# Experts' weights in 22 places for 17, column quarters in the gate and up products, and picks for one group of experts at a time

## The chip, the cores and the metric

The kernel runs on one core of a Trainium2 chip. Five engines work side by side and wait for each other through semaphores: TensorE (PE, matmuls into the eight banks of PSUM), VectorE (DVE), ScalarE (ACT), GpSimd (POOL) and SyncE (SP, which here issues all transfers, in order). The metric is the device time of one execution in microseconds. A smaller one is better.

## The reference

Two transformer blocks follow each other on 256 tokens of width 1024. The first has four feed-forward layers, a convolution and a latent attention; the second has a gated recurrence and an attention beside it, and then a mixture of 16 experts. The change lies in the experts. All weights are float32.

```python
def expert_choice_moe(h, w_router, w_gate, w_up, w_down):
    cap = EC_CAPACITY_FACTOR * length // N_EXPERTS        # 2 * 256 // 16 = 32 rows an expert
    aff = jax.nn.softmax((h @ w_router).astype(jnp.float32), axis=-1)
    gate, idx = lax.top_k(jnp.swapaxes(aff, 1, 2), cap)
    xe = h[bidx, idx]
    hid = jax.nn.silu(jnp.einsum("becd,edf->becf", xe, w_gate)) * jnp.einsum("becd,edf->becf", xe, w_up)
    ye = jnp.einsum("becf,efd->becd", hid, w_down) * gate[..., None].astype(h.dtype)
    return jnp.zeros_like(h).at[bidx, idx].add(ye)

        # behind the token mixing of the second block:
        x = x + g2 * expert_choice_moe(modulate(rms_norm(x, norm2_g[l]), sh2, sc2),
                                       w_router[l], w_exp_gate[l], w_exp_up[l], w_exp_down[l])
    return rms_norm(x, final_norm_g)
```

Each expert has three matrices of 1024 x 1024, so the experts' weights are 201 MB of the 427 MB that the kernel moves.

## The kernel before

Every engine has a program written out by hand, and SP's program is the order of all weights. A weight is loaded in pieces of 1 MB, [128 partitions x 2048], called slots or tiles. Up to the experts all pieces go through `ring`, six slots that are used in turn: PE raises the semaphore `slot_free` by one with the last matmul of a piece (`done`), and SP waits for that count before it loads piece n + 6 (`wait_free`). One SBUF region, `arena`, is laid out anew for every phase.

An expert has 12 tiles: four of the gate matrix, four of up, four of down (m = 0, 1, 2 in `product(m, j, src)`). Tile j holds rows 256 j to 256 j + 255, two to a partition (k = 0, 1). A product has 32 rows, so a matmul uses 32 of the array's columns, and four go to the four column groups of the array, into PSUM partitions 32 g on. Before the change they are the two k and the two halves of 512 output columns, so the results of the two k stand in different partitions: ScalarE copies one of them out of PSUM (`half_g_ready`, `half_u_ready`, `half_y_ready`) and VectorE adds the other.

Where expert tiles go before the change: 6 ring slots and 6 tiles `ahead` are used in turn (`EXP_SLOTS` is 12), and 5 `extra` tiles are used once, by the first five tiles of expert 1. That makes 17. SP loads two tiles into the ring while the branches run, waits for `merged_ready` (the two branches of the second block are added), loads the six ahead and then the rest as `w_out` frees ring slots, then the row of the final gain, and then tile after tile as places come free (`reused_load`).

The steps of the phase ahead, with the semaphores that the change uses: `hg_normed` (the recurrence's output is normed; its inputs are spent), `att_ready` (the attention's queries and keys are turned), the attention's blocks, two units of `branch` a and two of `branch` b (L1126), the four units of `w_out` (L1160), routing and seeding of the result in PSUM banks 0 to 3 (`h_seeded`), the choice of 32 tokens per expert (VectorE), then expert 0.

The chosen rows are gathered by matmuls with 0/1 `picks` (`gather`, L1213), for four experts at once (`GROUP`), into `x_exp`; in the kernel before this happens behind experts 1, 2 and 3 for the three later groups, and `x_cur` holds a copy of the rows of the expert in work. `spread` (L1221) turns the picks of one expert, scaled by its gates, and the last four matmuls of an expert (L1285) add its rows into banks 0 to 3. Behind the last expert the rows are squared and summed (ScalarE), scaled (VectorE) and stored. From expert 4 on all engines run a loop.

## Time and profile before

| | us |
|---|---|
| median of 3 runs | 1898.05 |
| lowest and highest | 1891.79, 1898.17 |
| the profiled execution's own time | 1893.91 |
| its span in the profile | 1892.1 |
| PE, PEld, DVE, ACT busy | 1733.2, 1376.9, 824.0, 673.2 |
| chain that ended last: PE, DMA, DVE, ACT | 77%, 14%, 4%, 3% |

The busy times are unions of the time in which the engine had an instruction in work. The chain is followed back from the last instruction, at each step to what released it. The profile cuts the span into 40 slices of 47.3 us and gives busy shares and transfer rates for each; the experts are the last ten. Rates of windows that are asked for are in GB/s, and a DMA share of about 1.0 says that all 16 DMA engines of the core worked all the time.

### The profile page before, as it was taken

The numbers are of one execution on the slowest core, as the hardware profiler recorded it, in microseconds if no ns is written. First come the engines' busy times: TensorE is split into PE (matmuls) and PEld (weight loads), VectorE is DVE, ScalarE is ACT, GpSimd is POOL, SyncE is SP. The second block draws the span as 40 slices with busy tenths as digits, with TensorE's granted clock in tenths as the row PEclk, the third lists the DMA queues.
The fourth block names the chain that finished last, engine by engine and source line by source line (L and its number), as shares of the span: only waits on it lengthen the run. The fifth ranks groups of instructions, "written<-read, shape, count | busy, mean of one in ns | idle before, by whom it ended". The sixth has DMA issues, their size and how long they took to land.

```text
span 1892.1 us, 28745 instructions
## 1 busy us (share of the span) xinstructions
PE 1733.2 (92%) x11907; PEld 1376.9 (73%) x11913; DVE 824.0 (44%) x1164; ACT 673.2 (36%) x976; POOL 10.7 (1%) x8
## 2 busy tenths in 40 slices
PE   8999999999999999999999999998998777767666
PEld 7999987999999999778999856886785332121212
DVE  6555697855566555134655504722422111111111
ACT  5444556644454443133444323315503221111111
POOL 0000010000000000000000000000000000000000
PEclk9999999999999999999999999999998887877777
DMA  9655455465546554544555452321179999999997
GB/s 300 226 175 186 157 187 185 134 200 177 183 151 200 180 187 149 159 130 142 193 191 185 156 157 88 112 90 67 45 285 376 397 422 422 422 422 422 422 422 325
DMA packets 200309, 427.12 MB, mean 226 GB/s; under 512 B 9187, under 2 KB 147861, under 8 KB 175668
## 3 DMA queue, kind: packets, MB, share of 16 engines
q1 hardware_dynamic: 200244, 426.19, 62.2%
q8 instruction: 48, 0.79, 0.2%
q14 instruction: 17, 0.14, 0.0%
HBM read 425.12 MB, written 1.05 MB: 225 GB/s over the span
## 4 chain that ended last, share of the span: by engine, by line
PE 77%; DMA 14%; DVE 4%; ACT 3%; SPq 1%; issue 1%; DVEq 0%; ACTq 0%
PE banks L621 14%; PE banks L622 14%; PE banks L623 14%; DMA ring<-in_w_exp_up 14%; PE banks L1247 4%; PE banks L995 4%; PE banks L971 3%; PE banks L792 2%; PE banks L744 1%; PE banks L1126 1%; PE banks L976 1%; PE banks L1160 1%; SPq L563 1%; PE banks L839 1%; PE banks L653 1%; PE banks L1213 1%
## 5 line engine op out<-in xcount | busy, mean ns | idle before, releaser
L621 PE MATMUL banks<-x_split,w_split 128*128 128x256 f32 x1600 | 457.1, 286 | 10.2 <-DVE x_split L1870 4.2
L622 PE MATMUL banks<-x_split,w_split 128*128 128x256 f32 x1600 | 453.4, 283 | 0.0
L623 PE MATMUL banks<-x_split,w_split 128*128 128x256 f32 x1600 | 453.3, 283 | 0.0
L1853 DVE TENSOR_TENSOR w_split<-ring,w_split 128x1024 fp32r<-128x1024 f32 x288 | 346.5, 1224 | 237.7 <-ACT w_split L1351 237.2
L1351 ACT ACTIVATE w_split<-ring 128x1024 fp32r<-128x1024 f32 x287 | 295.1, 1051 | 190.1 <-PE banks L623 188.2
L621 PEld LDWEIGHTS banks<-x_split,w_split 128*128 128x128 f32 x1600 | 307.8, 192 | 13.5 <-issue 6.0
L622 PEld LDWEIGHTS banks<-x_split,w_split 128*128 128x128 f32 x1600 | 307.7, 192 | 0.3
L623 PEld LDWEIGHTS banks<-x_split,w_split 128*128 128x128 f32 x1600 | 307.8, 192 | 0.0
L621 PE MATMUL banks<-hid_split,w_split 128*128 128x256 f32 x704 | 199.6, 284 | 0.0
L622 PE MATMUL banks<-hid_split,w_split 128*128 128x256 f32 x704 | 199.2, 283 | 0.0
L623 PE MATMUL banks<-hid_split,w_split 128*128 128x256 f32 x704 | 199.2, 283 | 0.0
L1247 PE MATMUL banks<-ring,arena 128*32 128x512 f32 x720 | 132.6, 834 | 42.2 <-DMA ring<-in_w_exp_up 35.1
L621 PEld LDWEIGHTS banks<-hid_split,w_split 128*128 128x128 f32 x704 | 135.1, 192 | 0.7 <-DVE hid_split L1922 0.7
L623 PEld LDWEIGHTS banks<-hid_split,w_split 128*128 128x128 f32 x704 | 135.1, 192 | 0.0
L622 PEld LDWEIGHTS banks<-hid_split,w_split 128*128 128x128 f32 x704 | 135.1, 192 | 0.0
L1247 PE MATMUL banks<-arena 128*32 128x512 f32 x728 | 107.6, 706 | 11.6 <-DMA arena<-in_w_exp_up 9.5
L1247 PEld LDWEIGHTS banks<-ring,arena 128*32 128x32 f32 x720 | 23.0, 132 | 108.8 <-DMA ring<-in_w_exp_up 71.9
L995 PE MATMUL banks<-xn,ring 128*128 128x256 f32 x448 | 99.4, 380 | 1.3 <-ACT arena L1612 0.7
L995 PEld LDWEIGHTS banks<-xn,ring 128*128 128x128 f32 x448 | 84.3, 190 | 13.9 <-issue 1.2
L1247 PEld LDWEIGHTS banks<-arena 128*32 128x32 f32 x728 | 26.4, 127 | 87.6 <-issue 56.1
L1400 ACT ACTIVATE hid_split<-gated 128x512 fp32r<-128x512 f32 x44 | 27.8, 632 | 150.4 <-DVE gated L1920 150.4
L2441 DVE TENSOR_TENSOR arena<-banks,arena 64x512 f32<-64x512 f32 x16 | 10.9, 683 | 152.8 <-ACT arena L1753 152.8
(371 smaller groups left out, 1893.5 us busy)
## 6 DMA issues: line engine op xcount, KB each, us to landing
ring<-in_ffn_w SPq DMA_DIRECT2D x131, 1024.0 KB, 5.3
arena<-in_w_exp_gate SPq DMA_DIRECT2D x58, 1024.0 KB, 24.4
ring<-in_w_exp_up SPq DMA_DIRECT2D x47, 1024.0 KB, 25.9
ring<-in_w_exp_down SPq DMA_DIRECT2D x45, 1024.0 KB, 24.5
ring<-in_w_mod SPq DMA_DIRECT2D x24, 1024.0 KB, 5.2
ring<-in_w_in SPq DMA_DIRECT2D x21, 1024.0 KB, 5.3
arena<-in_w_exp_down SPq DMA_DIRECT2D x19, 1024.0 KB, 26.0
arena<-in_w_exp_up SPq DMA_DIRECT2D x16, 1024.0 KB, 26.3
```

Source lines behind the costliest of these rows:

```text
L563: sp.dma_start(view, src).then_inc(full, 16)
L621: mm(out_, hi, moving(0), start=start, stop=False, **kw)
L622: mm(out_, hi, moving(1), start=False, stop=False, **kw)
L623: return mm(out_, lo, moving(0), start=False, stop=stop, **kw)
L653: last = mm(ps[:, bank, 0:n], ones[:, 0:P], squares[:, first + i, 0:n], start=(i == 0), stop=(i == k_tiles - 1))
L792: mm(ps[:, b, c:c + T], diag[:, q % DIAGS, :], conv_in[:, j, w:w + T], start=(w == 0), stop=(w == CONV_W - 1)).then_inc(sem("diag_used"), 1)
L971: last = mm(ps[:, b + o, :], slot(n)[:, k * 256 + o * P:k * 256 + o * P + P], xn[:, k, :], start=(k == 0), stop=(k == KD - 1))
L995: last = mm(ps[:, b, o * T:o * T + T], slot(n)[:, k * 256 + o * P:k * 256 + o * P + P], x_in[:, k, :], start=(k == 0), stop=(k == KD - 1))
L1247: last = mm(ps[g:g + 32, 4 + m, :], src(2 * j + k), w[:, k * D + 512 * half:k * D + 512 * half + 512], start=(j == 0), stop=(j == 3))
L1351: fn(half_part(n, o, 0), half_slot(n, o, columns), ACT.Copy).then_inc(sem("half_hi"), 1)
L1400: fn(hid_split[:, c % 2, 0, :, :], hidden[:, c % 2, :, :], ACT.Copy).then_inc(sem("hid_hi"), 1)
L1853: ins = dve.tensor_tensor(half_part(n, o, 1), half_slot(n, o, columns), half_part(n, o, 0).bitcast(F32), ALU.subtract)
```

## The change

The change has four parts.

- **Places.** The 12 + 5 places become 22 `tiles`, all used in turn by `tile_load(i)`: tile i of the 192 goes to place i % 22. Room for them comes from tensors whose contents are spent: `squares`, `gated`, `xn`, `h`, ten pieces of `arena` and the ring. The small tensors of the experts go to `roots` (std and rstd), `consts` and `att_stat`. The final gain's row goes last.
- **When they are asked for.** SP asks for tiles 0 and 1 behind `hg_normed`, 2 to 6 behind `att_ready`, 7 to 9 and 10 behind branch a, 11 and 12 behind branch b's units, 13 and 14 behind `merged_ready`, 15 to 18 as `w_out` frees ring slots, 19 and 20 behind its end and 21 behind `h_seeded`. The loads of `w_out` 2 and 3 now stand behind seven and ten of them.
- **Column quarters.** For gate and up a matmul has 256 output columns for 512, and the four column groups hold the four quarters; both k add up in PSUM. A tile has eight matmuls for four, the copy and the add of the halves are gone, and the activation works on [128 x 256]. Down has halves still, with its two k in different groups; their sum is left to the last four matmuls, which now contract 64 rows for 32, so the spread has 8 matmuls for 4 and the gate rows are 128 wide for 64.
- **Rows of one group.** `picks` holds four experts, computed anew by VectorE at experts 1, 5 and 9; the gather of a group comes behind experts 3, 7 and 11. `pick_cur` is computed by VectorE from the slots; `x_cur` is gone. All loops over experts are written out.

```diff
-        picks = r4.take(2 * TT, EXPERTS, CAP)
-        pick_cur, x_cur, spread_cur = r4.take(TT, CAP), r4.take(KD, CAP), r4.take(T)
-        choice = r4.take(6, T)
+        x_exp = laid(arena[:, 0:KD * GROUP * CAP], KD, GROUP * CAP)
+        choice = laid(roots[:, :], 4, T)
+        gate_e, hid_e = choice[:, 0, :], choice[:, 1, :]
+        y_e = choice[:, 2:4, :].rearrange("p a t -> p (a t)")
         work_a, work_b, chosen, slot_t = (choice[:, i, :] for i in range(4))
...
-        AHEAD = SLOTS
-        ahead = r4.take(AHEAD, SLOT)
-        once = r4.take(2, SLOT)
+        spent = consts[:, CONST["headsum"][0]:CONST["axial_sin"][1]]
+        picks = laid(spent[:, 0:TT * GROUP * CAP], TT, GROUP * CAP)
+        spread_cur = spent[:, 256:512]
+        hid_t = laid(spent[:, 512:768], KD, CAP)
+        pick_cur = laid(spent[:, 768:832], TT, CAP)
-        extra = [gated[:, :, :].rearrange("p a c -> p (a c)"), once[:, 0, :], once[:, 1, :],
-                 squares_flat[:, 0:SLOT], squares_flat[:, SLOT:2 * SLOT]]
-        EXTRA = len(extra)
-        EXP_SLOTS = SLOTS + AHEAD
-        REUSED = 12 * (EXPERTS - 1) - EXTRA
+        arena_tile = {a: arena[:, a:a + SLOT] for a in (1024, 3072, 5120, 7168, 9216, 11264, 13312, 15360, 17920, 19968)}
+        tiles = [squares_flat[:, 0:SLOT], gated[:, :, :].rearrange("p a c -> p (a c)")] + \
+                [arena_tile[a] for a in (7168, 9216, 11264, 17920, 19968, 1024, 3072, 5120)] + [squares_flat[:, SLOT:2 * SLOT]] + \
+                [ring[:, (N_EXPERTS + q) % SLOTS, :] for q in range(2)] + [arena_tile[a] for a in (13312, 15360)] + \
+                [ring[:, (N_EXPERTS + q) % SLOTS, :] for q in range(2, SLOTS)] + [xn_flat[:, 0:SLOT], xn_flat[:, SLOT:2 * SLOT]] + \
+                [h[:, :, :].rearrange("p k t -> p (k t)")]
+        TILES = len(tiles)
+        RING_TILES = (11, 12, 15, 16, 17, 18)
+        GAIN_TILE = 12 * (EXPERTS - 1)
+        gain_row = tiles[GAIN_TILE % TILES][:, 0:D]
...
-            def reused_load(u, more=None):
-                q, s = u % EXP_SLOTS, (u + EXTRA) % 12
-                used = u + 1 if u < EXP_SLOTS else u - EXP_SLOTS + 12 + EXTRA + 1
-                sp.wait_ge(slot_free, FIRST["experts"] + used + (0 if more is None else 12 * more))
-                expert_load(expert_view(q), s, 1 + (u + EXTRA) // 12, expert_full(q)[0], more)
-            for s in range(2):
-                wait_free(sp, FIRST["experts"] + s)
-                first_load(s)
+            def tile_load(i):
+                sp.dma_start(tiles[i % TILES], exp_tiles[i % 12][i // 12]).then_inc(tile_full(i % TILES)[0], 16)
+            def w_out_load(j):
+                cols(FIRST["w_out"] + j, w_out_2[0], 256 * j, 256, KD)
+            w_out_load(0)
+            w_out_load(1)
+            sp.wait_ge(sem("hg_normed"), 1)
+            for i in range(2):
+                tile_load(i)
+            sp.wait_ge(sem("att_ready"), 1)
+            for i in range(2, 7):
+                tile_load(i)
+            w_out_load(2)
+            sp.wait_ge(slot_free, FIRST["branch"] + 1)
+            for i in range(7, 10):
+                tile_load(i)
+            w_out_load(3)
+            sp.wait_ge(slot_free, FIRST["branch"] + 2)
+            tile_load(10)
+            for i in range(11, 13):
+                wait_free(sp, N_EXPERTS + RING_TILES.index(i))
+                tile_load(i)
             sp.wait_ge(sem("merged_ready"), 2)
-            for s in range(SLOTS, SLOTS + AHEAD):
-                first_load(s)
-            for s in range(2, SLOTS):
-                wait_free(sp, FIRST["experts"] + s)
-                first_load(s)
-                for b in ((0, 1, 2), (3, 4), (), ())[s - 2]:
-                    expert_load(extra[b], b, 1, sem("extra_in"))
+            for i in range(13, 15):
+                tile_load(i)
+            for i in range(15, 19):
+                wait_free(sp, N_EXPERTS + RING_TILES.index(i))
+                tile_load(i)
+            sp.wait_ge(slot_free, FIRST["w_out"] + 4)
+            for i in range(19, 21):
+                tile_load(i)
             sp.wait_ge(sem("h_seeded"), TT)
+            tile_load(21)
+            for i in range(TILES, 12 * EXPERTS):
+                sp.wait_ge(slot_free, N_EXPERTS + i - TILES + 1)
+                tile_load(i)
+            sp.wait_ge(slot_free, N_EXPERTS + GAIN_TILE + 1)
             sp.dma_start(gain_row, final_norm_g_2.partition_broadcast(P)).then_inc(sem("gain_row_in"), 16)
-            for u in range(EXP_SLOTS):
-                reused_load(u)
-            with sp.Fori(0, REUSED // EXP_SLOTS - 1) as i:
-                for u in range(EXP_SLOTS, 2 * EXP_SLOTS):
-                    reused_load(u, i)
-            for u in range(REUSED // EXP_SLOTS * EXP_SLOTS, REUSED):
-                reused_load(u)
...
-            def spread(more, e):
-                pe.wait_ge(sem("pick_cur_ready"), more + (e + 1))
+            def spread(e):
+                pe.wait_ge(sem("pick_cur_ready"), e + 1)
                 for t in range(TT):
-                    for g in (0, 32):
+                    for g in (0, 32, 64, 96):
                         last = mm(ps[g:g + 32, 7, T + t * P:T + t * P + P], pick_cur[:, t, :], ident, start=True, stop=True)
                 last.then_inc(sem("spread_turned"), 1)
...
+            def take(i):
+                full, first = tile_full(i % TILES)
+                pe.wait_ge(full, first + 16 * (i // TILES + 1))
+                return tiles[i % TILES]
+            def expert(e):
+                group, own = e // GROUP, slice((e % GROUP) * CAP, (e % GROUP) * CAP + CAP)
+                final = e == EXPERTS - 1
                 def product(m, j, src):
-                    w = take(4 * m + j)
+                    w = take(12 * e + 4 * m + j)
                     for k in range(2):
-                        for half in range(2):
-                            g = 32 * (2 * k + half)
-                            last = mm(ps[g:g + 32, 4 + m, :], src(2 * j + k),
-                                      w[:, k * D + 512 * half:k * D + 512 * half + 512],
-                                      start=(j == 0), stop=(j == 3))
+                        if m < 2:
+                            for q in range(4):
+                                last = mm(ps[32 * q:32 * q + 32, 4 + m, 0:256], src(2 * j + k),
+                                          w[:, k * D + 256 * q:k * D + 256 * q + 256],
+                                          start=(j == 0 and k == 0), stop=(j == 3 and k == 1))
+                        else:
+                            for half in range(2):
+                                g = 32 * (2 * half + k)
+                                last = mm(ps[g:g + 32, 6, :], src(2 * j + k),
+                                          w[:, k * D + 512 * half:k * D + 512 * half + 512],
+                                          start=(j == 0), stop=(j == 3))
                     done(last)
...
                     if j == 2 and not final:
-                        spread(more, e + 1)
-                        if group is not None:
-                            gather_group(group)
+                        spread(e + 1)
+                        if e % GROUP == GROUP - 1:
+                            gather_group(group + 1)
                     product(2, j, lambda k: hid_t[:, k, :])
...
+                wait_done(act, N_EXPERTS + 12 * e + 3)
+                fn(gate_e, ps[:, 4, 0:256], ACT.Silu).then_inc(sem("gate_act_ready"), 1)
...
-            with dve.Fori(0, EXPERTS) as e:
-                dve.wait_ge(sem("half_g_ready"), e + 1)
-                dve.tensor_tensor(gate_e[0:64, :], ps[0:64, 4, :], gate_e[0:64, :], ALU.add
-                                  ).then_inc(sem("gate_sum_ready"), 1)
-                dve.wait_ge(sem("half_u_ready"), e + 1)
-                dve.tensor_tensor(hid_e[0:64, :], ps[0:64, 5, :], hid_e[0:64, :], ALU.add).then_inc(sem("up_sum_ready"), 1)
-                dve.wait_ge(sem("up_sum_ready"), e + 1)
+            for e in range(EXPERTS):
+                if e % GROUP == 1 and e + GROUP < EXPERTS:
+                    dve.wait_ge(sem("x_exp_product"), 4 + 2 * (e // GROUP))
+                    picked(e // GROUP + 1)
                 dve.wait_ge(sem("gate_act_ready"), e + 1)
-                dve.tensor_tensor(hid_e[0:64, :], gate_e[0:64, :], hid_e[0:64, :], ALU.mult).then_inc(sem("hid_ready"), 1)
-                dve.wait_ge(sem("half_y_ready"), e + 1)
-                dve.tensor_tensor(y_e[0:64, :], ps[0:64, 6, :], y_e[0:64, :], ALU.add).then_inc(sem("y_sum_ready"), 1)
-                dve.wait_ge(sem("y_sum_ready"), e + 1)
-                dve.tensor_tensor(y_e[0:64, :], y_e[0:64, :], gate_rows[:, :], ALU.mult).then_inc(sem("y_ready"), 1)
+                wait_done(dve, N_EXPERTS + 12 * e + 7)
+                dve.tensor_tensor(hid_e, ps[:, 5, 0:256], gate_e, ALU.mult).then_inc(sem("hid_ready"), 1)
+                if e < EXPERTS - 1:
+                    dve.wait_ge(sem("spread_turned"), e + 1)
+                    pick_of(e + 1)
+                wait_done(dve, N_EXPERTS + 12 * e + 11)
+                dve.tensor_tensor(y_e, ps[:, 6, :], gate_rows, ALU.mult).then_inc(sem("y_ready"), 1)
```

On SP, the first place is between the second block's branches and the first reloads. Names are of tensors: `ring`, `arena`, `squares`, `gated`, `xn` and `h` hold places for tiles. Before:

```order
L441 DMA ring<-in_w_out 128x8x256 [waits slot_free] x4
L563 DMA ring<-in_w_exp_gate 128x2048 [waits slot_free] x2
L563 DMA arena<-in_w_exp_up 128x2048 [waits merged_ready]
L563 DMA arena<-in_w_exp_up 128x2048
L563 DMA arena<-in_w_exp_down 128x2048 x4
L563 DMA ring<-in_w_exp_gate 128x2048 [waits slot_free]
L563 DMA gated<-in_w_exp_gate 128x2048
L563 DMA arena<-in_w_exp_gate 128x2048 x2
L563 DMA ring<-in_w_exp_gate 128x2048 [waits slot_free]
L563 DMA squares<-in_w_exp_gate 128x2048
L563 DMA squares<-in_w_exp_up 128x2048
L563 DMA ring<-in_w_exp_up 128x2048 [waits slot_free] x2
```

and after the change, from behind the first two `w_out` loads:

```order
L564 DMA squares<-in_w_exp_gate 128x2048 [waits hg_normed]
L564 DMA gated<-in_w_exp_gate 128x2048
L564 DMA arena<-in_w_exp_gate 128x2048 [waits att_ready]
L564 DMA arena<-in_w_exp_gate 128x2048
L564 DMA arena<-in_w_exp_up 128x2048 x3
L444 DMA ring<-in_w_out 128x8x256 [waits slot_free]
L564 DMA arena<-in_w_exp_up 128x2048 [waits slot_free]
L564 DMA arena<-in_w_exp_down 128x2048 x2
L444 DMA ring<-in_w_out 128x8x256 [waits slot_free]
L564 DMA squares<-in_w_exp_down 128x2048 [waits slot_free]
L564 DMA ring<-in_w_exp_down 128x2048 [waits slot_free]
L564 DMA ring<-in_w_exp_gate 128x2048 [waits slot_free]
```

Seven tiles stand ahead of the third `w_out` load and ten ahead of the fourth, and thirteen are asked for ahead of the wait for `merged_ready`, which comes next; before, two are.

On PE, the second place is expert 3, from its last tile of up to the first half of down. Before (the last tile of up, turning the hidden rows at L1271, down at L1247, the spread at L1221 and the gather at L1213):

```order
L1247 MATMUL banks<-ring,arena 32x512 [waits slot_full_3]
L1247 MATMUL banks<-ring,arena 32x512 x3
L1271 MATMUL banks<-consts,arena 128x64 [waits spread_cur_ready,hid_ready]
L1271 MATMUL banks<-consts,arena 128x64 x3
L1247 MATMUL banks<-ring,arena 32x512 [waits slot_full_4,hid_t_ready]
L1247 MATMUL banks<-ring,arena 32x512 x3
L1247 MATMUL banks<-ring,arena 32x512 [waits slot_full_5]
L1247 MATMUL banks<-ring,arena 32x512 x3
L1221 MATMUL banks<-consts,arena 32x128 [waits pick_cur_ready]
L1221 MATMUL banks<-consts,arena 32x128 x3
L1213 MATMUL banks<-arena,tok 128x128 x16
L1247 MATMUL banks<-ring,arena 32x512 [waits slot_full_0]
```

and after:

```order
L1265 MATMUL banks<-arena 32x256 [waits tile_full_3]
L1265 MATMUL banks<-arena 32x256 x7
L1293 MATMUL banks<-consts,roots 128x128 [waits spread_cur_ready,hid_ready]
L1293 MATMUL banks<-consts,roots 128x128
L1271 MATMUL banks<-arena,consts 32x512 [waits tile_full_4,hid_t_ready]
L1271 MATMUL banks<-arena,consts 32x512 x3
L1271 MATMUL banks<-arena,consts 32x512 [waits tile_full_5]
L1271 MATMUL banks<-arena,consts 32x512 x3
L1229 MATMUL banks<-consts 32x128 [waits pick_cur_ready]
L1229 MATMUL banks<-consts 32x128 x7
L1221 MATMUL banks<-consts,tok 128x128 [waits pick_ready]
L1221 MATMUL banks<-consts,tok 128x128 x15
```

A tile of up has eight matmuls 32x256 where it had four 32x512, the turn has two for four, the spread eight for four, and the gather has the same 16; it now stands behind experts 3, 7 and 11 alone.

On VectorE, the third place is the work of one expert. Before, it is the body of the loop:

```order
L2431 UNCONDITIONAL_BRANCH
L2431 ISA
L2433 TENSOR_TENSOR arena<-banks,arena 64x512 [waits half_g_ready]
L2436 TENSOR_TENSOR arena<-banks,arena 64x512 [waits half_u_ready]
L2439 TENSOR_TENSOR arena<-arena 64x512 [waits gate_act_ready,up_sum_ready]
L2441 TENSOR_TENSOR arena<-banks,arena 64x512 [waits half_y_ready]
L2443 TENSOR_TENSOR arena<-arena 64x512 [waits y_sum_ready]
L2431 REGISTER_ALU
L2431 COMPARE_AND_BRANCH
```

and after, for expert 1, which also picks the group of experts 4 to 7 (the first two rows):

```order
L2392 TENSOR_TENSOR consts<-consts,arena 128x128 [waits x_exp_product]
L2392 TENSOR_TENSOR consts<-consts,arena 128x128
L2412 TENSOR_TENSOR roots<-banks,roots 128x256 [waits slot_free,gate_act_ready]
L2398 TENSOR_SCALAR consts<-consts,arena 128x32 [waits spread_turned]
L2398 TENSOR_SCALAR consts<-consts,arena 128x32
L2417 TENSOR_TENSOR roots<-banks,arena 128x512 [waits slot_free]
```

The three adds of 64x512 are gone, and two small picks have come between the product of gate and up and the scaling of the rows.

## Rows read from the trace of the kernel before

**Rows 1.** The page: the span, then rates in 40 slices, and queues.
```profile
span 1892.1 us, 28745 instructions
...
GB/s 300 226 175 186 157 187 185 134 200 177 183 151 200 180 187 149 159 130 142 193 191 185 156 157 88 112 90 67 45 285 376 397 422 422 422 422 422 422 422 325
...
q8 instruction: 48, 0.79, 0.2%
```

**Rows 2.** Windows of the experts' stretch; last columns granted clock, DMA share, GB/s.
```profile
core 0: us, PE busy (x) PEld busy (x) DVE busy (x) ACT busy (x) POOL busy (x), PEclk, DMA share, GB/s
1435.00:1440.00 5.00, 4.98 (x40) 3.22 (x40) 2.11 (x4) 2.27 (x6) 0.00 (x0) 1.00 0.38 97
1440.00:1470.00 30.00, 24.42 (x188) 9.99 (x184) 4.18 (x7) 8.42 (x18) 0.00 (x0) 0.89 0.99 406
...
1482.00:1492.00 10.00, 7.76 (x48) 1.96 (x44) 1.36 (x2) 1.93 (x5) 0.00 (x0) 0.83 0.83 312
...
1600.00:1860.00 260.00, 179.64 (x1040) 53.55 (x1036) 30.03 (x44) 31.35 (x70) 0.00 (x0) 0.75 1.01 422
...
1878.00:1880.00 2.00, 2.00 (x16) 0.51 (x12) 0.00 (x0) 0.00 (x0) 0.00 (x0) 0.63 0.43 176
```

**Rows 3.** Chain that ended last, in order of time: start us, us, what.
```profile
1365.15 27.84 PE banks L1126 x128
...
1395.55 19.26 PE banks L1160 x88
...
1462.22 7.05 PE banks L1247 x64
...
1502.96 4.46 PE banks L1213 x32
...
1538.45 8.61 PE banks L1247 x64
...
1597.30 1.11 PE banks L1247 x8
...
1627.11 1.98 PE banks L1247 x8
```

**Rows 4.** Timeline of SP's DMA issues from the output projection on.
```profile
1331.02 11.08 SPq L441 DMA_DIRECT2D ring<-in_w_out  x2
...
1386.10 7.25 SPq L563 DMA_DIRECT2D ring<-in_w_exp_gate  x2
...
1432.09 0.33 SPq L587 DMA_DIRECT2D h<-in_final_norm_g  x1
1438.23 4.60 SPq L563 DMA_DIRECT2D ring<-in_w_exp_up  x3
...
1467.71 2.04 SPq L563 DMA_DIRECT2D ring<-in_w_exp_up  x3
```

**Rows 5.** Timeline of VectorE before the attention's blocks.
```profile
1313.46 1.66 DVE L2300 SCALAR_TENSOR_TENSOR squares<-banks,vec_b,squares 128x256 f32<-128x256 f32 x4
...
1328.86 0.68 DVE L2326 TENSOR_TENSOR arena<-arena 128x512 f32<-128x512 f32 x1
```

**Rows 6.** Timeline of PE, four 32-column products with 256 moving columns.
```profile
1423.20 0.88 PE L1144 MATMUL banks<-h,pos_i 128*32 128x256 f32 x8
```

**Rows 7.** Waits from 1430 us on: us in total, times, longest.
```profile
PEld banks L1247 <- issue: 84.7, 179, 1.5
```

**Rows 8.** Timeline of the end, after the last product.
```profile
1881.72 0.59 ACT L1753 ACTIVATE arena<-banks 64x512 f32<-64x512 f32 x1 [5.45 <-PE banks L1247]
...
1883.06 0.68 DVE L2443 TENSOR_TENSOR arena<-arena 64x512 f32<-64x512 f32 x1
...
1886.52 0.16 DVE L2447 RECIPROCAL small<-small 128x1 f32<-128x1 f32 x1 [2.77 <-ACT small L1782]
```

**Rows 9.** DMA issues: KB each, median us to landing.
```profile
arena<-in_w_exp_gate SPq DMA_DIRECT2D x58, 1024.0 KB, 24.4
...
h<-in_final_norm_g SPq DMA_DIRECT2D x1, 512.0 KB, 5.6
```

202 lines of the change are left out of this document (73 added, 129 removed).

## Prediction

> **What bounds the kernel now.** I read the page first [rows 1]. Its line of rates says where the transfers bind: 422 GB/s in seven slices of 47.3 us, the 33rd to the 39th, and 45 GB/s in the 29th, before the experts begin. The windows say it again: from 1600 to 1860 us DMA is at 1.01 of its share and 422 GB/s while PE is busy 180 of 260 us [rows 2]. The chain of waits shows what follows whom: a product of expert e starts when its tile has landed, and the same tile of the next expert lands 29.81 us later (1597.30 to 1627.11) [rows 3]. Twelve tiles in 29.81 us are 2.484 us each, which is 1.0486 MB at 422 GB/s. So from about 1570 us the transfers set the pace, one tile in 2.484 us, whatever PE does. Before that PE was behind: experts 1 to 3 took 76.2 us (1462.22 to 1538.45), 25.4 us each [rows 3].
>
> So the end is: the moment from which DMA runs without a pause, plus the tiles then left times 2.484 us, plus every pause for want of a free place, plus the tail after the last byte. The timeline of SP's issues gives the first [rows 4]. The first product of expert 0 frees its place, and the first reload goes out at 1438.23 us. DMA has run dry by then: 97 GB/s from 1435 to 1440 us [rows 2], since all 17 places are full. The last byte comes at about 1878.8 us (176 GB/s between 1878 and 1880 is 0.83 us of full rate) [rows 2], and 192 - 17 = 175 tiles lie between. They need 434.7 us; the stretch from 1438.23 to 1878.8 is 440.6 us.
>
> **The five places.** By the first reload, 22 tiles can be in for 17. That leaves 170: 5 x 2.484 = 12.4 us less of transfer in the bound stretch. It needs two things. First, all 22 must have landed by 1438 us. The two early tiles need hg_normed (VectorE, done 1315.1 us) and the next five att_ready (1329.5 us) [rows 5], but SP is in order and stands at w_out's second load until about 1341.8 us (1331.02 + 11.08 less the short issue) [rows 4]. So seven tiles go at 1342 us and, with that w_out load ahead, are through by about 1362 (8 x 2.484 = 19.9). Branch a's units end at 1372.1 and 1379.1 us (27.84 us for four from 1365.15) [rows 3]. W_out 2 and three tiles go at 1372.1, w_out 3 and a tile at 1379.1, two ring tiles at 1386.0 and 1393.0 us, two tiles when the merged rows are ready (1395.55, where PE's output projection starts) [rows 3]. Four follow that projection's units, about 7.0 us each (19.26 us for 2.75 of them), two more its end, and one h_seeded, for which the gain row waits today and goes out at 1432.09 us [rows 4]. From 1395.5 us on nine tiles, 22.4 us of transfer, have 42.7 us. I expect all 22 in at about 1436 us. The moved loads pass w_out 2 and 3 on SP: w_out 2 is issued when its place is free in both kernels, behind an empty queue, and w_out 3 behind 4 transfers, of which three quarters are done. It lands before 1388 us and PE wants it near 1416: 28 us of cover.
>
> Second, the start at 1438.23 us must not move. The gate rows are 128 wide for 64, the same column count and count of matmuls; the VectorE steps ahead of the first product are the same ones. I cost this at nothing; if the wider copy were twice as long (it is 0.6 us like L1753's [rows 8]) it would still be beside the picks.
>
> **The places that came back late.** Today's five extra places are used once, so the ring has 12. Expert 0 frees 12, and the reload after those goes out only at 1467.71 us [rows 4], because expert 1's first five tiles free nothing. DMA pays twice: 406 GB/s over 1440 to 1470 (30 x 16/422 = 1.1 us) and 312 over 1482 to 1492 us (10 x 110/422 = 2.6 us) [rows 2]. With 22 places all in turn, expert 1's first tiles are reloaded at once. At 1462 us PE has freed 12 and DMA has moved 9.6; five more come free by 1467. I take the whole 3.7 us; the lower bound is 0.
>
> **Fewer steps per expert.** With column quarters the two halves need no copy and no add. On the path of the end that is ScalarE's L1753 and VectorE's L2441: from 1881.72 to 1883.06 us [rows 8], 1.34 us out of the tail. The same removal in the gate and up steps, the x_cur and pick copies, and the gather once in four experts instead of after 1, 2 and 3 (4.46 us [rows 3]) make PE faster where DMA sets the pace. I cost these at nothing; their cover is the 29.81 us per expert. The eight matmuls of a gate or up tile have the columns of the four before (8 x 256 = 4 x 512), all in four column groups. Before, eight tiles take 7.05 us [rows 3], 0.88 each. The nearest row of small ones is L1144: four with 32 columns by 256 in 0.88 us, start and drain in it [rows 6]. The bounds for a tile are 0.88 and 1.76 us. At the upper one an expert is 25.4 + 7.05 - 4.5 (gather) - 2.5 (two copies and two adds of some 0.6 and 0.7 us) = 25.5 us, under 29.8. I take the lower, for DMA either way.
>
> The gain row moves from an idle moment to behind the last tile. It is half a tile, 1.2 us, and landed 5.6 us after its issue [rows 9]. VectorE wants it at 1886.52 - 1.34 us, 6.3 us after the last byte on today's times [rows 8]: hidden, by 0.7 us if all 5.6 came after that byte.
>
> **Sum.** 12.4 + 3.7 + 1.3 = 17.5 us off 1892.1: a span of 1874.6, and 1876.4 us beside the profiled execution's 1893.91. The median of the runs shown, 1898.05, lies 4.1 us above that one execution, so on the median it would be 1880.5. I put the time between, 1878.5 us.
>
> The Trainium skill (DMA: Bandwidth & Descriptors, Bandwidth) gives the memory side as the bound of a load, about 358 GB/s a core; a tile would cost 2.93 us by it and the five places 14.6 us, an estimate. The trace disagrees, with 422 GB/s held for 260 us [rows 2], and the row decides.
>
> **Rivals.** *Only the places count* (0.13): the pauses stay, because PE frees places in bursts. For it: PE stands still for spread and gather. Against: the burst of eight tiles covers 19.9 us. It gives 1878.5 + 3.7 = 1882 us.
> *The places aren't full in time* (0.08): SP is in order, and one late wait (h_seeded, or the fourth w_out unit) holds all behind it. Each tile that isn't in by 1438 us gives back 2.48 us; at five the change does not do what it says, and 3.7 + 1.3 = 5 us are left, 1891 us, no change by measure. Against it is the 20 us of slack counted above.
> *Small tiles make PE the bound* (0.04; slower): a round of four 256-column matmuls may not overlap the next. It decides from (29.8 - 25.4 + 7.05 + 7.0) / 16 = 1.15 us a round, against 0.88 in the row and half of that if they overlap. At the lower clock of 1.2 GHz, if rounds stood alone at 1.76 us, an expert would need 25.4 - 14.05 + 28.2 = 39.5 us, and 15 of them 146 us more: about 2025 us. Granted clock was 0.75 in the bound stretch [rows 2], a mixture of both levels, and PE reached it waiting; a PE that never waits was at 1.00 (1435 to 1440).
> *Code comes late* (0.03; slower): PE's 16 experts are written out, where eleven ran in a loop. The instruction queue moved 0.79 MB in 48 packets [rows 1], and weights in a full queue take 24.4 us to land [rows 9]. If one code packet per expert waited so long, less the 4.4 us to spare per expert, it would cost 20 us each, 240 us over twelve: about 2120 us. Against it: experts 1 to 3 are straight code today beside a full queue, and the longest wait of this kind is 1.5 us [rows 7].
> The Trainium skill (Runtime: NRT & Kernel Launch, Instruction fetch mechanics) has code fetched ahead page by page in a straight run, and a taken branch as what stalls; by that the written-out experts cost nothing, and the 1.5 us agrees.
>
> **Chances and range.** The forecast, 15 to 20 us less: 0.66. More than that, from an earlier end of the routing or a faster tail: 0.06. With the rivals that is 1.00. Half a per cent is 9.5 us, about what a measurement of this kernel tells from no change. Faster by more than that: 0.66 + 0.06 + 0.13 and a quarter of the second rival, 0.87. Within it: 0.08, with part of the mild end of PE's pace. Slower: 0.05. The range runs from 1871 (20.5 us less on the lower basis, and 2.4 for the unknown) to 1887.5 us (10.6 us less on the median).
>
> **What would show it.** Right: SP's first reload near 1438.2 us with 22 tiles out before it, seven at 1342 us; 422 GB/s without a dent from 1441 us on; a last byte at about 1862.7 us; equal tiles of late experts still 29.8 us apart; a tail of about 11.9 us from the last byte to the end for 13.2. Wrong: dents at 1482 us or in an expert with a gather; a first reload after 1440 us; tiles spaced by more than 29.8 us with DMA under 1.0, which is PE's pace or code; DVE waiting for the gain row at the end.

## The result and the profile after

The changed kernel took 1877.39 us (median of 4 runs, 1876.69 to 1879.12), the one before 1898.11 us on the same chip (4 runs). The ratio, estimated from the runs, is 0.9899, with a 95% interval of 0.9877 to 0.9922, so the kernel is 1.0% faster. The changed kernel is called after below, the other one before. Forecast were 1878.5 us, 1871 to 1887.5. The profiled execution has a span of 1875.0 us, where 1874.6 were forecast.

From the page of the changed kernel: the span, the rates in 40 slices and the instruction queue. It is to be read beside [rows 1].

```profile
span 1875.0 us, 30152 instructions
...
GB/s 296 235 163 195 157 181 200 120 197 182 185 153 190 188 180 139 173 164 113 182 199 179 157 202 68 113 69 89 184 287 246 424 426 425 425 425 425 425 425 335
...
q8 instruction: 66, 1.08, 0.2%
```

The rate is at its upper level one slice earlier, from the 32nd slice on, and that level is 425 and not 422 GB/s. The tiles asked for early are moved ahead of it, which shows in the 29th slice (184 for 45 GB/s). The windows say it closer (columns as in [rows 2]):

```profile
1435.00:1440.00 5.00, 4.88 (x52) 3.81 (x56) 0.47 (x3) 2.09 (x6) 0.00 (x0) 1.00 0.44 126
1440.00:1450.00 10.00, 8.91 (x144) 5.21 (x137) 0.84 (x3) 3.57 (x7) 0.00 (x0) 1.00 0.94 371
1440.00:1470.00 30.00, 26.19 (x374) 13.01 (x363) 3.46 (x10) 4.72 (x10) 0.00 (x0) 1.00 0.99 408
1482.00:1492.00 10.00, 9.19 (x128) 4.15 (x120) 0.69 (x1) 0.77 (x2) 0.00 (x0) 1.00 1.01 423
1600.00:1840.00 240.00, 166.10 (x1572) 63.32 (x1572) 12.66 (x34) 15.21 (x40) 0.00 (x0) 0.81 1.01 425
```

The pause between 1482 and 1492 us is gone, 423 GB/s for 312 [rows 2]. The one at the start is not: 408 GB/s over 1440 to 1470 us against 406, and all of the loss lies in the first ten microseconds (371; before has 370 there).

SP's issues (start us, us), which answer to [rows 4]:

```profile
1342.54 0.58 SPq L564 DMA_DIRECT2D squares<-in_w_exp_gate  x1
...
1373.11 0.58 SPq L564 DMA_DIRECT2D arena<-in_w_exp_up  x1
...
1408.34 14.91 SPq L564 DMA_DIRECT2D ring<-in_w_exp_up  x3
...
1431.98 0.33 SPq L564 DMA_DIRECT2D h<-in_w_exp_down  x1
1438.41 0.33 SPq L564 DMA_DIRECT2D squares<-in_w_exp_down  x1
```

The h tile is tile 21, the last of the 22, and the row under it is the first reload, at 1438.41 us for 1438.23. From here to the start of the last product DMA sets the time, so this "stretch" is compared in all that follows. The chain shows the equal products (the last tile of down) of the last four experts:

```profile
1776.13 1.11 PE banks L1271 x8
...
1805.79 1.11 PE banks L1271 x8
...
1835.39 1.98 PE banks L1271 x8
...
1864.76 1.11 PE banks L1271 x8
```

They are 29.54 us apart on average. Over ten experts it is 29.81 us, as is shown below. The last product starts at 1864.76 us, 15.8 us earlier than before (1880.59), and the stretch is 426.35 us for 442.36. From that product to the end it is 10.2 us for 11.5, as the timeline of the end shows. It is to be read beside [rows 8]: no row of ScalarE stands between the product and VectorE's any more.

```profile
1864.76 1.06 PE L1271 MATMUL banks<-ring,consts 128*32 128x512 f32 x8 [1.16 <-DMA ring<-in_w_exp_down]
1865.89 0.69 DVE L2417 TENSOR_TENSOR roots<-banks,arena 128x512 f32<-128x512 f32 x1 [8.43 <-PE banks L1271]
...
1866.64 1.99 PE L1307 MATMUL banks<-roots,consts 64*128 64x512 f32 x8 [0.81 <-DVE roots L2417]
...
1869.36 0.16 DVE L2421 RECIPROCAL small<-small 128x1 f32<-128x1 f32 x1 [2.77 <-ACT small L1756]
```

### The profile page after: what moved, and what is told of

It is laid out like the page before. It is cut to its first block, busy times and chain, and to the rows that moved or that the text cites. A ratio compares the mean times of both kernels' runs of the same rounds, so it can differ in the third digit from the quotient of the medians.

```text
span 1875.0 us, 30152 instructions
## 1 busy us (share of the span) xinstructions
PE 1715.6 (92%) x13001; PEld 1387.8 (74%) x13001; DVE 792.9 (42%) x1150; ACT 633.6 (34%) x897; POOL 10.7 (1%) x8
## 4 chain that ended last, share of the span: by engine, by line
PE 74%; DMA 19%; DVE 4%; ACT 2%; SPq 0%; issue 0%; DVEq 0%; ACTq 0%
PE banks L629 15%; PE banks L631 14%; PE banks L630 14%; DMA arena<-in_w_exp_up 6%; PE banks L1003 4%; DMA ring<-in_w_exp_up 4%; PE banks L979 3%; DMA arena<-in_w_exp_down 3%; PE banks L800 2%; PE banks L1265 2%; PE banks L752 1%; PE banks L1134 1%; PE banks L984 1%; DMA h<-in_w_exp_up 1%; DMA gated<-in_w_exp_up 1%; DMA gated<-in_w_exp_down 1%
## 5 line engine op out<-in xcount | busy, mean ns | idle before, releaser
L2412 DVE TENSOR_TENSOR roots<-banks,roots 128x256 f32<-128x256 f32 x16 | 6.8, 425 | 273.4 <-PE banks L1265 273.4
L1265 PE MATMUL banks<-arena 128*32 128x256 f32 x1008 | 74.5, 433 | 32.4 <-DMA arena<-in_w_exp_up 22.9
L1265 PEld LDWEIGHTS banks<-arena 128*32 128x32 f32 x1008 | 30.7, 119 | 77.3 <-DMA arena<-in_w_exp_up 36.4
L1881 DVE TENSOR_TENSOR gated<-banks,roots 128x512 f32<-128x512 f32 x88 | 60.3, 685 | 34.2 <-PE banks L631 34.0
L2417 DVE TENSOR_TENSOR roots<-banks,arena 128x512 f32<-128x512 f32 x16 | 11.1, 692 | 132.4 <-PE banks L1271 132.4
## 6 DMA issues: line engine op xcount, KB each, us to landing
ring<-in_w_exp_down SPq DMA_DIRECT2D x17, 1024.0 KB, 26.4
```

The costliest lines, as they stand in the source:

```text
L1265: last = mm(ps[32 * q:32 * q + 32, 4 + m, 0:256], src(2 * j + k), w[:, k * D + 256 * q:k * D + 256 * q + 256], start=(j == 0 and k == 0), ...
L1881: return dve.tensor_tensor(dst, ps[:, bank + c % 2, :].rearrange("p (k t) -> p k t", t=T), scale, ALU.mult)
```

## The experiments

One view is used for all. For each kernel the windows were read from the first reload on, and the time that DMA lost in a part of the stretch is its length times (1 less rate over the steady rate). "Start" is the first 14 us of the stretch, "mid" the next 76, "last 9" its last 9 us; in between nothing is lost in any kernel. The steady rate is a whole number of GB/s, so the column "at steady rate" is good to 0.5 us. "End" is from the last product to the end of the span.

```
                          ratio to before       first    last     stretch  at steady   lost in us       end
                          (95% interval)        reload   product           rate (GB/s) start mid  last 9
before                    1                     1438.23  1880.59  442.36   435.2 (422)  2.6  2.7  1.8   11.5
after                     0.9899 .9877-.9922    1438.41  1864.76  426.35   421.5 (425)  2.5  0    2.3   10.2
after_again               0.9906 .9890-.9922    1438.39  1864.78  426.39   421.4 (425)  2.7  0.2  2.1   11.2
hold17                    0.9977 .9966-.9988    1442.97  1881.70  438.73   433.9 (425)  2.7  0    2.1   10.2
hold17_ring12             0.9964 .9952-.9976    1442.47  1881.93  439.46   434.0 (425)  2.6  0    2.9   12.1
late_asking               0.9941 .9928-.9954    1441.97  1875.15  (DMA never dry)                      10.9
gain_late                 0.9895 .9880-.9910    1438.78  1865.04  426.26   420.7 (425)  2.0  0    3.6   11.2
copies_back               0.9914 .9898-.9930    1437.90  1864.73  426.83   421.5 (425)  2.5  0.2  2.7   11.8
slow22                    0.9911 .9895-.9928    1438.13  1864.45  426.32   421.6 (425)  1.9  0    2.8   11.5
slow17                    0.9984 .9975-.9994    1438.24  1877.73  439.49   434.0 (425)  2.7  0    2.8   11.6
slow12                    0.9986 .9975-.9997    1438.54  1880.52  441.98   433.8 (425)  1.9  3.6  2.6   12.5
before_sp_flat            1.0005 .9993-1.0016   1438.40  1881.25  442.85   435.4 (422)  2.6  2.7  2.2   11.6
before_pe_flat            1.0007 .9995-1.0018   1437.96  1880.31  442.35   436.2 (421)  2.8  0.4  3.0   11.5
before_turn17             0.9998 .9988-1.0009   1436.91  1879.27  442.36   436.3 (421)  2.5  0    3.6   11.5
```

In the traces of hold17, hold17_ring12 and late_asking the phases ahead of the experts took some 4 us longer (SP's first load of w_out goes out at 1335.92 us in hold17, at 1331.42 in after), so the stretch says more than the moment at which something happens.

A rate counts bytes, and a product waits for a whole tile. So a second table has the landings of tiles, read from the traces. The last up tile of expert 5 is tile 67 of 0 to 191. "Up to tile 67" is the time from the first reload to its landing, less 2.485 us, the pace of before, for each tile reloaded up to it (51 with 17 places, 46 with 22). It is what the tiles came late, the first landing included. The next column is the time of the 124 tiles from there to the last one.

```
                 up to tile 67   tile 67 to the last   landing of the last tile
                 late by, us     us                    to the last product, us
before           7.45            308.13                0.05
after            4.14            307.86                0.04
after_again      4.14            307.90                0.04
hold17           4.03            307.92                0.05
hold17_ring12    4.81            307.87                0.05
late_asking      10.91           307.91                0.04
gain_late        3.98            307.92                0.05
copies_back      4.59            307.89                0.04
slow22           3.98            307.98                0.04
slow17           4.79            307.92                0.04
slow12           7.32            307.88                0.04
before_sp_flat   7.86            308.21                0.05
before_pe_flat   5.47            309.63                0.51
before_turn17    5.28            309.64                0.70
```

The products show the same. Tile 67 and the last up tile, 120 tiles on, in before:

```profile
1572.45 1.94 PE L1247 MATMUL banks<-ring,arena 128*32 128x512 f32 x8 [1.42 <-DMA ring<-in_w_exp_up]
...
1870.67 1.06 PE L1247 MATMUL banks<-ring,arena 128*32 128x512 f32 x8 [1.43 <-DMA ring<-in_w_exp_up]
```

and in after:

```profile
1556.90 1.93 PE L1265 MATMUL banks<-gated,arena 128*32 128x256 f32 x16 [0.53 <-DMA gated<-in_w_exp_up]
...
1854.97 1.93 PE L1265 MATMUL banks<-ring,arena 128*32 128x256 f32 x16 [0.53 <-DMA ring<-in_w_exp_up]
```

That is 298.22 and 298.07 us. At 425 GB/s for 422 it would be 2.1 us less, so the higher rate lands no tile earlier.

**Five places fewer** (hold17).

```diff
             def tile_load(i):
+                if i >= 17:
+                    sp.wait_ge(slot_free, N_EXPERTS + i - 17 + 1)
                 sp.dma_start(tiles[i % TILES], exp_tiles[i % 12][i // 12]).then_inc(tile_full(i % TILES)[0], 16)
```

> The changed kernel with everything but five of its places: tile 17 and all later ones wait for one more release each, so that never more than 17 tiles are in SBUF or on their way; the result is the same. Theory (each place is one transfer less in the bound stretch): the span grows by 5 x 2.48 = 12.4 us over the changed kernel's 1875.0, to about 1887.4, and the ratio to the kernel before is about 0.996. First reload still near 1438.4 us, 175 tiles behind it. Rival A (the gain is the pace of PE or the shorter chain, places matter little): the span stays within 3 us of 1875.0. Rival B (17 places in turn also bring pauses back): more than 15 us.

The stretch is 12.4 us longer than after, 2.48 us for each place, and the time by the two ratios 14.8 us, good to some 5. Places are worth what the theory says. Rival A is out, and rival B by the trace, which has no pause in the middle; the times alone could not rule it out.

**The same, with five places used once** (hold17_ring12).

```diff
-                    sp.wait_ge(slot_free, N_EXPERTS + i - 17 + 1)
+                    sp.wait_ge(slot_free, N_EXPERTS + i - (17 if i < 29 else 12) + 1)
```

> As the kernel with 17 places, and from tile 29 on a load waits for the release of the tile 12 before it, not 17: so five places are used once, as in the kernel before. The result is the same. Theory (the places that came back late cost DMA two pauses): 3.7 us more than the kernel with 17 in turn, a span of about 1891, with a dent in the rate near 1470 and between 1482 and 1492 us. Rival (the pauses were caused by PE's slower experts before the change, not by the places): no dent at 1482 us, the same span as with 17 in turn, within 1 us.

A miss. There is no pause, and the stretch is 0.7 us longer, not 3.7. With 12 places in turn this PE starves nothing.

**22 places, asked for late** (late_asking).

```diff
             sp.wait_ge(sem("hg_normed"), 1)
+            sp.wait_ge(sem("att_ready"), 1)
+            w_out_load(2)
+            w_out_load(3)
+            sp.wait_ge(slot_free, FIRST["branch"] + 2)
             for i in range(2):
                 tile_load(i)
-            sp.wait_ge(sem("att_ready"), 1)
-            for i in range(2, 7):
+            sp.wait_ge(sem("merged_ready"), 2)
+            for i in range(2, 11):
                 tile_load(i)
-            w_out_load(2)
-            sp.wait_ge(slot_free, FIRST["branch"] + 1)
-            for i in range(7, 10):
-                tile_load(i)
-            w_out_load(3)
-            sp.wait_ge(slot_free, FIRST["branch"] + 2)
-            tile_load(10)
             for i in range(11, 13):
                 wait_free(sp, N_EXPERTS + RING_TILES.index(i))
                 tile_load(i)
-            sp.wait_ge(sem("merged_ready"), 2)
             for i in range(13, 15):
                 tile_load(i)
```

> The changed kernel with its 22 places, but tiles 0 and 1 are asked for behind branch b's first units and tiles 2 to 12 behind the merged branches; the two later loads of the output projection go ahead of all tiles. The result is the same. Theory: 20 tiles then have to be moved from 1397 us on without a pause, 49.7 us at 2.484 us each, to about 1447, which is 8 us behind the moment (1438.4 us) at which the changed kernel starts its reloads; less its start-up dent of about 1 us and what else differs, the span grows by 5 to 8 us, to 1880 to 1883. Rival (the places alone matter, asking early is not needed): the same span within 1.5 us.

By the ratio it is 8.0 us more than after, good to some 5; in the trace the last product starts 6.8 us later, the 3.56 us of its later first reload taken off. The places alone are not enough. The window from 1435 to 1440 us shows why, 424 GB/s for 126:

```profile
1435.00:1440.00 5.00, 3.88 (x42) 3.42 (x41) 3.44 (x12) 1.81 (x4) 0.00 (x0) 1.00 1.01 424
```

The places were not full by the first reload; the transfers that should have been done by then still ran.

**The row of the gain asked for late** (gain_late).

```diff
-            sp.wait_ge(slot_free, N_EXPERTS + GAIN_TILE + 1)
+            sp.wait_ge(slot_free, N_EXPERTS + 12 * EXPERTS - 1)
```

> The changed kernel, with the row of the final gain asked for when the last tile but one has been used (near 1864 us) and not behind the last tile (1843 us). The result is the same. In the changed kernel the transfer rate falls in steps over the last 6 us, 287, 254, 197, 197, 160, 37 GB/s from 1860 us on. Theory A (the row's packets share the engines with the last tiles and slow them): the last product starts 1 to 3 us earlier, and the span is 1872 to 1874 if the row still lands before VectorE wants it at 1869.5 us. Theory B (the tiles land at the pace of the slowest of the 16 engines, and the others are merely done sooner): the last product starts within 0.5 us of where it did, and the span is the same or up to 1 us longer, if the row then comes late.

The time is as theory B has it: the stretch is the same (426.26 us) and the ratio too. The bytes of the row are not what holds the last tile; that the slowest engine does is not shown. The row landed in 3.3 us, in time. The kernel's end is 1.0 us longer than after's for another reason, told below.

**Copies back, and a slow PE** (copies_back, slow22, slow17, slow12). Shown is the chain of the expert's rows; gate and up get the same pair.

```diff
+                wait_done(act, N_EXPERTS + 12 * e + 11)
+                fn(y_e, ps[:, 6, :], ACT.Copy).then_inc(sem("aff_exp"), 1)
...
-                wait_done(dve, N_EXPERTS + 12 * e + 11)
-                dve.tensor_tensor(y_e, ps[:, 6, :], gate_rows, ALU.mult).then_inc(sem("y_ready"), 1)
+                dve.wait_ge(sem("aff_exp"), TT + 3 * e + 3)
+                dve.tensor_tensor(y_e, ps[:, 6, :], y_e, ALU.max).then_inc(sem("slots_chosen"), 1)
+                dve.wait_ge(sem("slots_chosen"), 1 + 3 * e + 3)
+                dve.tensor_tensor(y_e, y_e, gate_rows, ALU.mult).then_inc(sem("y_ready"), 1)
```

and for the three slow ones, which have 22, 17, and 17 places with 12 in turn (by the edits above):

```diff
+                        if e in (1, 2):
+                            pe.wait_ge(sem("pick_ready"), 2)
+                            for k in (0, 1, 2, 3, 4, 5, 6, 7, 0, 1, 2, 3):
+                                gather(k, 4 + k // 4, (k % 4) * P)
```

> The changed kernel with ScalarE's copy out of PSUM and a VectorE step put back into each of the three chains of every expert (gate, up, rows), as the kernel before has them; the VectorE step takes the larger of a value and its own copy, so the result is the same. Theory: 15 of the 16 experts hide it under the transfers (the pace of the late experts stays at 29.5 to 29.8 us), and the last one pays in the tail, 1.0 to 1.5 us between its last product and the end: a span 1 to 2 us over the changed kernel's, when the start of the execution is the same. Rival (the steps stand on the path of every expert): 2 to 4 us for each, 30 us or more in all.

The stretch is 0.5 us longer, so 15 experts hide the steps. In the last one the copy starts at 1865.86 us and the scaling at 1867.22: 1.4 us are paid there. The rival is out.

> As the kernel with the copies back, and behind experts 1 and 2 PE also does 24 gather matmuls whose products nobody reads (some 6 us each), so that experts 1 to 3 take PE about as long as before the change, 23 to 26 us for the 15.75 us of the changed kernel; 22 places in turn. The result is the same. With 22 places in turn even this PE should starve nothing: no window between 1460 and 1540 us under 415 GB/s, and the same time as the kernel with the copies back within 1.5 us. Rival (PE's faster experts gave part of the gain whatever the places): 2 to 4 us more.

Nothing starves, and the stretch is that of after to 0.03 us (0.5 us under copies_back), with experts 1 to 3 at 25.4 to 27.3 us. The faster PE gives nothing by itself when there are 22 places.

> The same slow PE with 17 places, all in turn; the result is the same. If places in turn are what removed the pauses, as predicted, there is no dent between 1470 and 1500 us and the last product starts within 1 us of the one of the fast kernel with 17 places (12.4 us behind the changed kernel's). If it was PE's pace that removed them, a dent of 1 to 4 us comes back here too.

> The same slow PE with 17 places of which five are used once, so 12 in turn; the result is the same. The fast PE with these places had no pause at 1482 us and ended its transfers only 0.7 us later than with 17 in turn, where 3.7 were predicted. Theory now: the pauses of the kernel before needed both, 12 places and a slow PE, so that here a dent of 2 to 4 us comes back between 1470 and 1500 us (rate under 350 GB/s in ten of these microseconds), 2 to 4 us more than the fast kernel with these places. Rival (they came from something else in the kernel before): no dent.

Windows of slow17, then of slow12:

```profile
1480.00:1490.00 10.00, 7.83 (x76) 3.11 (x72) 1.39 (x2) 0.98 (x2) 0.00 (x0) 0.83 1.01 424
1490.00:1500.00 10.00, 8.11 (x104) 3.73 (x96) 1.69 (x5) 1.57 (x4) 0.00 (x0) 0.86 1.02 427
```

```profile
1480.00:1490.00 10.00, 7.83 (x76) 2.90 (x72) 1.38 (x2) 0.98 (x2) 0.00 (x0) 0.83 0.89 333
1490.00:1500.00 10.00, 8.10 (x108) 3.77 (x104) 1.70 (x5) 1.57 (x4) 0.00 (x0) 0.88 0.97 369
```

So the pause needs both, 12 places in turn and a slow PE, and either cure removes it. In this kernel it costs 2.5 us of the stretch (441.98 less 439.49), and all of it lies up to tile 67 (7.32 less 4.79). The medians of slow17 and slow12 can't tell 2.5 us apart; the traces can.

**Loops of the kernel before written out** (before_sp_flat, before_pe_flat).

```diff
-            with sp.Fori(0, REUSED // EXP_SLOTS - 1) as i:
-                for u in range(EXP_SLOTS, 2 * EXP_SLOTS):
-                    reused_load(u, i)
+            for u in range(EXP_SLOTS, REUSED // EXP_SLOTS * EXP_SLOTS):
+                reused_load(u)
```

```diff
-            with pe.Fori(0, EXPERTS - GROUP - 1) as i:
+            for i in range(EXPERTS - GROUP - 1):
```

> The kernel before, with SP's loop over the later tiles written out; nothing else, the result is the same. Open is why all kernels built on the changed one move 425 GB/s while the transfers bind, for 422 before, and yet land their last tile no earlier, because the rate falls to about 205 GB/s, half of it, for the last 4 us. Theory S (SP's loop, whose addresses come from a register, makes the difference): here 425 GB/s and the last 4 us at about half the rate. Theory C (it is the code that PE must fetch): 422 GB/s and a full rate up to 2 us before the last tile, as before. Last product within 1 us of 1880.6 in both, when the start of the execution is the same.

> The kernel before, with PE's loop over experts 4 to 14 written out; the result is the same. Theory S: 422 GB/s and a full rate up to 2 us before the last tile. Theory C (the fetched code takes time of some of the 16 DMA engines, so that these end later): more packets in the instruction queue than the 48 of before, 425 GB/s, and the last 4 us at about half the rate. It is also the rival of the prediction in which code comes late, by itself: if it holds, the pace of the late experts grows from 29.81 us and the time by up to 20 us an expert; if not, the time is that of the kernel before within 0.2%, and the longest wait for PE's next instruction stays at about 1.5 us.

Both move 421 to 422 GB/s, so neither theory explains 425. SP's loop changes nothing. With PE written out the instruction queue has 58 packets, and of theory C one half came, a fall to half the rate (369, 197, 188 and 131 GB/s in the microseconds before DMA is through); but the time is the same, and the longest wait for PE's next instruction too:

```profile
PEld banks L1247 <- issue: 82.8, 168, 1.5
```

This kernel also had nearly no pause in the middle (0.4 us), as its expert 0 ran 3 us faster, at a granted clock of 0.96 for 0.69 between 1450 and 1460 us, and still a stretch of 442.35 us.

**The kernel before with places in turn** (before_turn17). It contains SP's and PE's loops written out, and two of VectorE's semaphores are exchanged for free ones.

```diff
-            for u in range(EXP_SLOTS):
-                reused_load(u)
-            with sp.Fori(0, REUSED // EXP_SLOTS - 1) as i:
...
+            for i in range(PLACES, 12 * EXPERTS):
+                sp.wait_ge(slot_free, FIRST["experts"] + i - PLACES + 1)
+                expert_load(turn_view(i % PLACES), i % 12, i // 12, turn_full(i % PLACES)[0])
```

> The kernel before with its 17 places all in turn (the five extra ones are reloaded too); SP's and PE's loops are written out for it; PE's experts, copies and gathers are as they were. The result is the same. With the slow PE added to the changed kernel, places in turn removed a pause at 1480 to 1495 us and let the last product start 2.8 us earlier; so here the last product should start at 1877.5 to 1878.3 us instead of 1880.6, and the span be about 1889.5. Rival: the kernel before with PE's loop written out had a pause of only 0.5 us for 2.7 and ended no earlier, so something else of the kernel before (its 422 GB/s for 425) holds the end at 1880.3 to 1881.3 us whatever the pause.

The pause is gone, 422 GB/s in both windows from 1480 to 1500 us, and nothing is gained: 442.36 us, ratio 0.9998. The rival's outcome came (with the 1.3 us by which the first reload is earlier, 1880.6 us). Up to tile 67 the kernel is 2.2 us ahead of before. Of these, 1.5 us are lost on the way to the last tile (309.64 us for 308.13), without a pause, and 0.7 behind it. before_pe_flat loses the same 1.5 us, and after, whose PE is written out too, does not; the cause is open. The timeline of the last expert shows the other 0.7:

```profile
1868.73 1.93 PE L1252 MATMUL banks<-ring,arena 128*32 128x512 f32 x8 [1.42 <-DMA ring<-in_w_exp_up]
...
1870.73 0.59 ACT L1737 ACTIVATE arena<-banks 64x512 f32<-64x512 f32 x1 [8.84 <-PE banks L1252]
...
1871.36 0.68 DVE L2437 TENSOR_TENSOR arena<-banks,arena 64x512 f32<-64x512 f32 x1 [10.13 <-ACT arena L1737]
...
1872.07 0.68 DVE L2440 TENSOR_TENSOR arena<-arena 64x512 f32<-64x512 f32 x1
...
1872.81 1.97 PE L1276 MATMUL banks<-consts,arena 64*128 64x64 f32 x8 [2.15 <-DVE arena L2440]
...
1874.82 0.38 ACT L1741 ACTIVATE arena<-banks 128x256 f32<-128x256 f32 x1 [3.49 <-PE banks L1276]
...
1875.25 5.05 PE L1252 MATMUL banks<-ring,arena 128*32 128x512 f32 x32 [0.47 <-ACT arena L1741]
...
1879.27 1.03 PE L1252 MATMUL banks<-ring,arena 128*32 128x512 f32 x8
```

From the last up tile to the first down product it takes 6.5 us, then four tiles run almost without a wait. The last one landed at 1878.57 us, 0.7 us before its product starts. In the last 4 us of the stretch DMA moves only 100 GB/s, while it moves 206 in the same part of after:

```profile
1875.25:1879.25 4.00, 4.00 (x24) 1.03 (x28) 0.00 (x0) 0.00 (x0) 0.00 (x0) 0.64 0.24 100
```

So here the chain of copies and adds sets the end and not the last tile. In before the two tie: the last tile lands at 1880.54 us, just before its product, and PE is at work without a gap from the first down product (1876.32 us) on.

**The changed kernel once more** (after_again).

> The changed kernel once more, beside the one above on the same chip: a ratio near 0.990, the last product within 0.5 us of 1864.8 us when its start is the same, and again about 205 GB/s, half the rate, in the last 4 us before it.

The ratio is 0.9906 and the last product starts at 1864.78 us. DMA moves 200 to 220 GB/s in the last 4 us before it, half the rate as expected.

## Why the prediction was right, step by step

**The bound and the start.** Right: the first reload is at 1438.41 us, all 22 tiles out before it, seven of them from 1342.54 us on. The 22 places are full and DMA falls dry again (126 GB/s), which confirms that they were in by about 1437.

**The five places, 12.4 us.** Right: 12.4 us with the fast PE (hold17 against after), 13.2 with the slow one (slow17 against slow22). Asking early is needed for it, and worth 7 to 8 us of it.

**The places that came back late, 3.7 us.** Right in its place and nearly in its size, but the cure was only in part the one named. Up to tile 67 the tiles come 3.3 us less late (4.14 us for 7.45), which is where the prediction saw its two dents. One of them, the 1.1 us between 1440 and 1450 us, stayed. It is the start: PE frees its first places 2.1 us apart, as it gathers between them (1438.41, 1440.55 us). The other, 2.6 us, went away, but places in turn are one of two cures: 12 in turn have no pause either with this PE (hold17_ring12), nor have 17 in turn with a slow one (slow17). In the kernel before, places in turn give 2.2 us up to tile 67 and nothing at the end (before_turn17). From that kernel to after another 1.1 us lie in the same part (5.28 less 4.14), which no row prices. So the 3.7 us of the sum met 3.3 partly by luck: a dent that stayed was made up for by something that was not in the working.

The account of the stretch, by landings: five tiles 12.4, the tiles up to tile 67 3.3, the 124 tiles behind it 0.3. That makes 16.0, the measured 442.36 less 426.35, where the prediction has 12.4 and 3.7. The rate, 425 GB/s for 422, is no term of it.

**The last byte.** The prediction puts it at about 1878.8 us in the kernel before. That is where DMA would end if it held its full rate; it still moves 82 GB/s between 1879 and 1880 us, and the last tile lands at 1880.54, just before its product. Counted in its way (the start of the last product less the loss in the last 9 us), the transfers of after end at 1862.4 us, where 1862.7 were forecast, and 12.6 us follow, where 11.9 were. So on that measure the transfers gave 16.4 us for 16.1 and the tail 0.7 for 1.3, as the fall of the rate at the end took 0.5 us more.

**Fewer steps per expert.** From the last product to the end they gave 1.3 us of 1.34 in the profiled execution. It is not certain, though: in after_again the last 8 matmuls (L1307) took 3.68 us for 1.99, at a granted clock of 0.52 for 1.00 (1.2 GHz for 2.4), and the end 11.2 us. In front of them PE had waited for tiles in both, 1.16 us for the last one in after and 1.38 in after_again. Four of the six executions without the copies show the long form, with 10.9 to 12.1 us from the last product to the end, so the tail gives between 1.3 us and nothing. Elsewhere the steps are hidden, as forecast (copies_back). Experts that no transfer holds up need 15.75 us for 24.9 to 26.4, far better than the 18 to 25 us in the working. Not seen was that in the last expert the chain from its last up tile to its first down product nearly counts as well: it takes 5.65 us in the kernel before, where it ties with the last tile, and 4.2 us now (1854.97 to 1859.21), so that the last product waits for its tile again.

**Small tiles.** Eight tiles of 64 matmuls take 7.09 us, beside the 7.05 of [rows 3]: the lower bound was the right one.

```profile
1456.19 7.09 PE banks L1265 x128
```

**Code.** The longest wait of this kind is 1.5 us, as before [rows 7], and before_pe_flat took the rival away by itself. The Trainium skill (Runtime: NRT & Kernel Launch, Instruction fetch mechanics) has a straight run fetched ahead; the trace agrees.

**The gain row** landed only 22.9 us after its issue, where the prediction took 5.6, but it was issued early enough (1843.0 us), and VectorE never waited for it.

```profile
arena<-in_final_norm_g SPq DMA_DIRECT2D x1, 512.0 KB, 22.9
```

**The basis.** The span fell by 17.1 us, where 17.5 were forecast. The median lies 2.4 us above the span, where 3.9 us had been allowed (1878.5 less 1874.6). The two misses have opposite signs, and that the median is only 1.1 us off the forecast owes something to this.

Three things are open: why DMA runs further ahead of the landed tiles in the kernels with quarters (425 GB/s for 421 to 422; neither loop explains it, and no kernel changed the places' layout or the matmuls alone), why the kernel before loses 1.5 us behind tile 67 once PE is written out, and what the 1.1 us without a price are.

## What to carry to other kernels

Where transfers bind, count tiles: each place that is full when the bound stretch begins takes one tile's time off it, provided the load is asked for early enough to be in. Judge a stream by when the same tile lands, not by its bytes per microsecond: 425 GB/s for 422 moved no tile forward. A dent in the rate is no sum by itself; look at whether its removal moves the last tile, and then whether the chain behind the last tiles is short enough to use it. A repair that is tested alone on the old kernel can show nothing and still be part of a gain.

## What the runs showed of the hardware

In these kernels the end of the stream of tiles is ragged. In after the rate falls to half about 4 us before the last product, and the DMA share, the time that the 16 engines are in work, falls with it:

```profile
1860.76:1864.76 4.00, 2.84 (x20) 0.47 (x13) 0.00 (x0) 0.00 (x0) 0.00 (x0) 0.78 0.49 206
```

A pause in the middle does not even it out: the last 9 us lose 2.2 us in before_sp_flat with a pause of 2.7, 2.6 us in slow12 with one of 3.6, and 2.1 us in after_again without one.

More bytes in a microsecond do not mean that tiles land sooner. Between the products of tile 67 and of the last up tile 120 tiles land, 125.8 MB. The DMA view of these stretches, q1 being SP's queue and q8 the fetching of code, first in before, then in after:

```profile
DMA packets 17279, 125.84 MB, mean 422 GB/s; under 512 B 1920, under 2 KB 1920, under 8 KB 1920
q1 hardware_dynamic: 17278, 125.82, 101.4%
q8 instruction: 1, 0.02, 0.0%
```

```profile
DMA packets 17388, 126.77 MB, mean 425 GB/s; under 512 B 1930, under 2 KB 1930, under 8 KB 1930
q1 hardware_dynamic: 17371, 126.50, 100.9%
q8 instruction: 16, 0.26, 0.3%
```

The stretches are 298.22 and 298.07 us long. Of the 0.9 MB more in after, 0.2 are code and 0.7 are bytes of tiles that land later. That fits engines that drift apart, each at its own place in the stream, and so does an end at half the rate; it was not shown engine by engine. The Trainium skill (DMA: Bandwidth & Descriptors, Two DMAs through the same engine are not ordered) has it that nothing orders DMAs across the 16 engines, which would allow it; no run here shows the order.

This kernel, on one core, held 425 GB/s over 240 us. The Trainium skill (HBM Reference, Specifications (TRN2)) gives about that for a core that streams alone, and 358 as its share when both cores of a pair do; the prediction set only the smaller figure against the trace.
